# Differential attention interleaved with its projections: heads 0-3 between chunks, output product in contraction halves, bias sum and maximum in one operation

## What is computed

```python
proj = h @ w_in                                  # 1024 -> q, k, v of 1024 each
q = rms_norm(q.reshape(B, S, 8, 2, 64), g[0]) * 64 ** -0.5
k = rms_norm(k.reshape(B, S, 8, 2, 64), g[1])
p1 = softmax(einsum('bhqd,bhkd->bhqk', q1, k1) + bias)
p2 = softmax(einsum('bhqd,bhkd->bhqk', q2, k2) + bias)
out = einsum('bhqk,bhkv->bhqv', p1 - lam * p2, vh)
out = rms_norm(out, subln_g) * (1.0 - lam_init)  # over each head's 128 columns
return out.reshape(B, S, 1024) @ w_out           # added to x
```

## Time and profile before

| | us |
|---|---|
| median of 3 runs | 2019.35 |
| lowest and highest of them | 2018.79, 2026.88 |
| the profiled execution, its own time | 2024.16 |
| span of that execution, first to last instruction | 2022.4 |
| busy in the span: PE, DVE, ACT | 1924.5, 1226.9, 992.1 |
| mean granted TensorE clock | 0.986 |

### The profile page before, as it was taken

One profiled execution on the slowest core, in us unless ns is written; L12 is line 12 of the kernel. 1 busy time (PEld: TensorE's weight loads), 2 busy tenths in 40 slices (PEclk: granted clock), 3 DMA queues, 4 the chain that ended last, 5 costly groups with the idle time before them and its releaser, 6 DMA issues.

```text
span 2022.4 us, 26323 instructions
## 1 busy us (share of the span) xinstructions
PE 1924.5 (95%) x9384; PEld 1613.5 (80%) x9384; DVE 1226.9 (61%) x1633; ACT 992.1 (49%) x1479; POOL 64.2 (3%) x94
## 2 busy tenths in 40 slices
PE   9999989999999998799999999978989999989998
PEld 7887777888788886688888887867878788878886
DVE  5554786555555578655555566887565556655564
ACT  5444665544544455654453546633355543334444
POOL 1000000000000000000000001010000012100000
PEclk9999999999999999999999999989989999999999
DMA  7656334666685653166565555422135544336453
GB/s 224 188 185 185 120 115 153 184 188 188 189 257 186 186 172 125 57 184 182 189 200 167 183 167 176 148 77 70 40 107 170 159 146 126 104 105 210 153 187 115
DMA packets 215891, 316.88 MB, mean 157 GB/s; under 512 B 16658, under 2 KB 115208, under 8 KB 215536
## 3 DMA queue, kind: packets, MB, share of 16 engines
q1 hardware_dynamic: 212704, 306.76, 49.2%
q0 software_dynamic: 3024, 8.75, 1.3%
q10 hardware_dynamic: 64, 0.02, 0.0%
HBM read 314.41 MB, written 3.16 MB: 157 GB/s over the span
## 4 chain that ended last, share of the span: by engine, by line
PE 86%; DVE 8%; ACT 3%; issue 2%; DMA 0%; SPq 0%; DVEq 0%; ACTq 0%
PE acc L754 50%; PE acc L759 24%; PE tp L714 4%; DVE w_lo L1998 1%; PE tp L1163 1%; PE tp L870 1%; PE mx L1163 1%; DVE arena L2478 1%; ACT w_hi L1381 1%; DVE arena L2242 1%; PE mx L1302 1%; PE mx L1303 1%; DVE x L2069 1%; DVE arena L2402 1%; PE mx L1218 0%
## 5 line engine op out<-in xcount | busy, mean ns | idle before, releaser
L1998 DVE TENSOR_TENSOR w_lo<-w_raw,w_hi 128x1024 fp32r<-128x1024 f32 (+1 forms) x589 | 712.6, 1217 | 518.3 <-ACT w_hi L1381 516.3
L1381 ACT ACTIVATE w_hi<-w_raw 128x1024 fp32r<-128x1024 f32 (+1 forms) x589 | 612.9, 1048 | 568.7 <-PE acc L759 546.7
L754 PE MATMUL acc<-w_hi,norm_hi 128*128 128x512 f32 x1488 | 475.0, 401 | 4.1 <-DVE norm_lo L2017 3.5
L754 PE MATMUL acc<-w_hi,norm_lo 128*128 128x512 f32 x1488 | 461.8, 392 | 0.0
L759 PE MATMUL acc<-w_lo,norm_hi 128*128 128x512 f32 x1488 | 396.4, 389 | 0.0
L754 PEld LDWEIGHTS acc<-w_hi,norm_lo 128*128 128x128 f32 x1488 | 281.6, 190 | 59.8
L759 PEld LDWEIGHTS acc<-w_lo,norm_hi 128*128 128x128 f32 x1488 | 278.8, 188 | 58.0
L754 PEld LDWEIGHTS acc<-w_hi,norm_hi 128*128 128x128 f32 x1488 | 274.2, 191 | 58.9 <-issue 3.1
L754 PE MATMUL acc<-w_hi,inner_hi 128*128 128x512 f32 (+1 forms) x864 | 267.3, 391 | 4.0 <-DVE inner_lo L2017 2.5
L754 PE MATMUL acc<-w_hi,inner_lo 128*128 128x512 f32 (+1 forms) x864 | 262.9, 386 | 0.0
L759 PE MATMUL acc<-w_lo,inner_hi 128*128 128x512 f32 (+1 forms) x864 | 226.9, 385 | 0.0
(11 more groups left out here) (309 smaller groups left out, 1351.5 us busy)
## 6 DMA issues: line engine op xcount, KB each, us to landing
w_raw<-in_ffn_w_gu SPq DMA_DIRECT2D x352, 256.0 KB, 3.0
w_raw<-in_ffn_w_down SPq DMA_DIRECT2D x88, 512.0 KB, 4.6
w_raw<-in_pool_w_in SPq DMA_DIRECT2D x64, 512.0 KB, 3.8
w_raw<-in_gdn_w_in SPq DMA_DIRECT2D x48, 512.0 KB, 3.9
w_raw<-in_pool_w_out SPq DMA_DIRECT2D x32, 512.0 KB, 4.4
w_raw<-in_mla_w_in SPq DMA_DIRECT2D x26, 512.0 KB, 3.7
w_raw<-in_gla_w_in SPq DMA_DIRECT2D x24, 512.0 KB, 3.6
w_raw<-in_diff_w_in SPq DMA_DIRECT2D x24, 512.0 KB, 4.3
```

The source lines that it names most:

```text
L754: pe.matmul(acc_of(g, i, part, tok, 0, w), t[:, tile * SEQ + tok * P:tile * SEQ + (tok + 1) * P], b_hi, start=t is hi and k + kk == 0, sto ...
L1381: act.activation(slot(w_hi, g, i, p, 0, n), slot(w_raw, g, i, p, 0, n), ACT.Copy).then_inc(S["rounded"], 1)
L1998: dve.tensor_tensor(slot(w_lo, g, i, p, 0, n), slot(w_raw, g, i, p, 0, n), slot(w_hi, g, i, p, 0, n).bitcast(F32), ALU.subtract).then_inc( ...
```

## The change

`diff` now has six single blocks, q0, k0, v0, q1, k1, v1, where 0 are the columns of heads 0-3. After v0 the eight units of heads 0-3 run; PE puts one chunk of q1, k1 or v1 between the transposes and the values of each. The steps for q1 and k1 stand between the steps of these units on ACT and DVE. In this half there is one bank for scores and one shared by transposed probabilities and output. The output product is ordered by halves of the contraction: chunks 0 to 3 need heads 0-3 only. Heads 4-7 follow with three score banks; the roots, normalisation and transposes of the outputs are made for four heads at a time. The bias sum and the maximum become one operation for each of the two score matrices of a unit, which writes the negated sum and its minimum; the exponential takes scale -1. In the diff, cut to its core, "..." marks what is left out.

```diff
+        if turn_by is not None:
+            self.chunks.sort(key=lambda c: (c[1] // turn_by, c[0], c[1]))
...
+def halves(name, w, kt, cols, per, turn_by):
+
+    def source(first):
+        def piece(i, k, nk):
+            ap = w[k * P:(k + nk) * P, first:first + cols].rearrange("(t k) n -> k t n", k=P)
+            return [(lambda s: s[:, 0:nk * cols].rearrange("p (t n) -> p t n", t=nk), ap)]
+        return piece
+    return Gemm(name, 1, [(kt, cols, per, source(n * cols)) for n in range(2)], turn_by=turn_by)
...
-    return [linear("diff.qk", w, KD, BANK, 4, 2),
-            linear("diff.v", w, KD, BANK, 2, 2, first=2 * DM, evac="act_evac"),
-            linear("diff.out", t["diff_w_out"][0], KD, BANK, TT, 2)]
+    return [linear("diff.q0", w, KD, BANK, 1, 2),
+            linear("diff.k0", w, KD, BANK, 1, 2, first=DM),
+            linear("diff.v0", w, KD, BANK, 1, 2, first=2 * DM, evac="act_evac"),
+            linear("diff.q1", w, KD, BANK, 1, 2, first=BANK),
+            linear("diff.k1", w, KD, BANK, 1, 2, first=DM + BANK),
+            linear("diff.v1", w, KD, BANK, 1, 2, first=2 * DM + BANK, evac="act_evac"),
+            halves("diff.out", t["diff_w_out"][0], KD, BANK, 2, KD // 2)]
...
         def diff_bank(n):
 
-            return bank(mx, n % 4) if n % 4 < 2 else bank(tp, n % 4 - 2)
+            return bank(mx, 0) if n < diff_half else (bank(mx, 0), bank(tp, 0), bank(tp, 1))[(n - diff_half) % 3]
+
+        def diff_pt_bank(n):
+
+            return bank(mx, 1, 0, SEQ) if n < diff_half else bank(acc, 2 * G["diff.v1"].odd(0) + n % 2, 0, SEQ)
+
+        def diff_o_bank():
+
+            return bank(mx, 1, SEQ, P)
...
+            def finish_halves(g, xt, need):
+
+                st = following.get(g.name.split(".")[0])
+                for p in (g.n // 2, g.n // 2 + 1):
+                    product(g, 0, xt, part=0, only=p, need=need)
+                product(g, 0, xt, part=1, only=g.n - 2, need=need)
+                if st:
+                    turn_x(st, (0, 1))
+                product(g, 0, xt, part=1, only=g.n - 1, need=need)
...
                 def scores(n):
                     h, it = units[n]
-                    if n >= DIFF_AHEAD:
-                        pe.wait_ge(S["diff_s_taken"], n + 1 - DIFF_AHEAD)
+                    if 0 < n <= diff_half:
+                        pe.wait_ge(S["diff_s_taken"], n)
+                    elif n >= diff_half + 3:
+                        pe.wait_ge(S["diff_s_taken"], n - 2)
...
                 def probs_turned(n):
                     pe.wait_ge(S["diff_p_ready"], n + 1)
-                    if n >= 2:
+                    if 0 < n < diff_half:
+                        pe.wait_ge(S["diff_o_taken"], n)
+                    elif n >= diff_half + 2:
                         pe.wait_ge(S["diff_pt_ready"], n - 1)
                     for kt in range(TT):
-                        last = pe.transpose(bank(acc, n % 2, kt * P, P), p[:, n % 2 * SEQ + kt * P:n % 2 * SEQ + (kt + 1) * P], ident[:, :])
+                        last = pe.transpose(diff_pt_bank(n)[:, kt * P:(kt + 1) * P], p[:, n % 2 * SEQ + kt * P:n % 2 * SEQ + (kt + 1) * P],
+                                            ident[:, :])
                     see["diff_pt_turned"].up(last)
                 def values(n):
                     h, it = units[n]
                     pe.wait_ge(S["diff_pt_ready"], n + 1)
-                    if n >= 2:
-                        pe.wait_ge(S["diff_o_taken"], n - 1)
+                    if n >= diff_half:
+                        pe.wait_ge(S["diff_o_taken"], n)
                     for kt in range(TT):
-                        last = pe.matmul(bank(acc, 2 + n % 2, 0, P), pt[:, n % 2 * SEQ + kt * P:n % 2 * SEQ + (kt + 1) * P],
+                        last = pe.matmul(diff_o_bank(), pt[:, n % 2 * SEQ + kt * P:n % 2 * SEQ + (kt + 1) * P],
...
+                product(q0_g, 0, norm_t, need=need)
+                product(k0_g, 0, norm_t, between=lambda p: turn_block(0) if p == 2 else None)
+                product(v0_g, 0, norm_t, between=lambda p: turn_block(1) if p == 2 else None)
+                turned(see["tp_ready"].n - 1)
                 pe.wait_ge(S["diff_vec_ready"], 1)
+                scores(0)
+                product(q1_g, 0, norm_t, only=0)
+                wait_evacuated(pe, v0_g, 0)
+                filling = [*[(q1_g, p) for p in range(1, 4)], *[(k1_g, p) for p in range(4)], (v1_g, 0)]
+                for n in range(diff_half):
+                    if n + 1 < diff_half:
+                        scores(n + 1)
+                    probs_turned(n)
+                    g, p_n = filling[n]
+                    product(g, 0, norm_t, only=p_n)
+                    values(n)
+                    if n == 5:
+                        turn_block(2)
+                product(v1_g, 0, norm_t, only=1)
+                turn_heads(0)
+                product(v1_g, 0, norm_t, only=2)
+                turn_block(3)
+                product(v1_g, 0, norm_t, only=3)
+                turned(see["tp_ready"].n - 1)
+                for n in range(diff_half, diff_half + 3):
                     scores(n)
+                product(out_g, 0, inner_t, part=0, only=0, need=need_heads)
+                wait_evacuated(pe, v1_g, 0)
+                for n in range(diff_half, 2 * diff_half):
                     probs_turned(n)
+                    if n == diff_half + 1:
+                        product(out_g, 0, inner_t, part=0, only=1, need=need_heads)
+                    if n + 3 < 2 * diff_half:
+                        scores(n + 3)
+                    values(n)
+                product(out_g, 0, inner_t, part=1, only=2, need=need_heads)
+                product(out_g, 0, inner_t, part=1, only=3, need=need_heads)
+                turn_heads(1)
+                finish_halves(out_g, inner_t, need_heads)
...
+                plain_units(6)
+                feed.to(q1_g.chunk0 + 4)
+                exps(0)
+                for n in range(diff_half):
+                    take_probs(n)
+                    feed.to(q1_g.chunk0 + n + 5)
+                    if n + 1 < diff_half:
+                        exps(n + 1)
+                    if n == 3:
+                        block(2)
+                    if n == 4:
+                        block_root()
+                        act.activation(warm[:, :], eps[:, :], ACT.Exp)
+                    if n == 7:
+                        block(3)
+                    take_o(n)
+                root(0)
+                block_root()
+                act.activation(warm[:, :], eps[:, :], ACT.Exp)
+                feed.to(out_g.chunk0 + 1)
+                for u in range(2):
+                    hi_part(inner_t, 2 * u, lambda k: ROWS["subln"])
+                feed.to(out_g.chunk0 + 2)
+                plain_units(2)
+                feed.to(out_g.chunk0 + 3)
+                scaled_evac(v1_g, 0, diff_t["v"], DM, ACT.Copy, first=BANK)
+                for n in range(diff_half, diff_half + 3):
                     exps(n)
+                feed.to(out_g.chunk0 + 4)
+                for n in range(diff_half, 2 * diff_half):
                     take_probs(n)
+                    if n == diff_half + 1:
+                        feed.to(out_g.chunk0 + 5)
+                    if n + 3 < 2 * diff_half:
+                        exps(n + 3)
+                    if n + 3 == 2 * diff_half:
+                        act.activation(warm[:, :], eps[:, :], ACT.Sqrt)
+                    take_o(n)
+                root(1)
+                feed.to(out_g.chunk0 + 7)
+                for u in range(2, 4):
                     hi_part(inner_t, 2 * u, lambda k: ROWS["subln"])
+                finish_halves(out_g)
...
-                    b = bias[:, (it * DIFF_H + h) * SEQ:(it * DIFF_H + h + 1) * SEQ].rearrange("p (a k) -> p a k", a=1)
-                    dst = s[:, ring * BANK:(ring + 1) * BANK].rearrange("p (m k) -> p m k", m=2)
-                    see["diff_s_taken"].up(dve.tensor_tensor(dst, diff_bank(n).rearrange("p (m k) -> p m k", m=2),
-                                                             b.to_broadcast([P, 2, SEQ]), ALU.add))
-                    see["diff_s_taken"].wait(dve)
-                    see["diff_max_ready"].up(dve.tensor_reduce(stat[:, 16 + 2 * ring:18 + 2 * ring], dst, AX_X, ALU.max, negate=True))
+                    b = bias[:, (it * DIFF_H + h) * SEQ:(it * DIFF_H + h + 1) * SEQ]
+                    for m in range(2):
+                        last = dve.tensor_tensor_reduce(out=s[:, ring * BANK + m * SEQ:ring * BANK + (m + 1) * SEQ],
+                                                        in0=diff_bank(n)[:, m * SEQ:(m + 1) * SEQ], in1=b, scale=-1.0, scalar=3.0e38,
+                                                        op0=ALU.add, op1=ALU.min, accum_out=stat[:, 16 + 2 * ring + m:17 + 2 * ring + m])
+                    see["diff_s_taken"].up(last)
...
+                feed.before_evac(q0_g, 0)
+                evac(0)
```

(54 more changed lines are left out.)

210 lines of the change are left out of this document (94 added, 116 removed).

## The result

| | before | after |
|---|---|---|
| time, median (range) | 2022.5 us (2018.2 to 2026.9), 10 runs | 2031.0 us (2028.2 to 2040.3), 10 runs |
| ratio, 95% interval | | 1.0048 [1.0031, 1.0065] |
| span of the profiled execution | 2022.4 | 2027.6 |
| this stage in it | 144.07 | 154.60 |

The forecast was 2031. The change makes the kernel slower by 0.3 to 0.65%, 6 to 13 us. The interval lies on both sides of the 0.5% at which the prediction parted "slower" (chance 0.53) from "no change" (0.38), so which of the two it is stays open.

A forecast was written before the change was run, and what follows sets the result against it. PE bounds the kernel, so only its idle time can be won. Waits rise from 26.1 to 34.6 us (+8.5), clock adds 3.0: +11.5 on 2019.35 gives 2031, own range 2029.4 to 2034, wider range 2016 to 2038.

The forecast's parts named there:

- 2 unit 3 to 4: First half: PE waits 3.0 us for take_o(3), queued on ScalarE behind block(2), which waits for VectorE's evacuation.
- 3 unit 4 to 5: First half: PE waits 3.4 us for take_o(4), behind two table loads, a wait for P(5), and a root.
- 7 turn_block(3): Between the halves: the turning of block 3 and its copies make PE wait 1.1 us.
- units 8 to 12: Second half: a unit takes 3.6 us against 2.37, with 2.0 of waiting in each, 10.0 in all.
- last three units: End of second half: transposes, copy and values follow with nothing between, plus a 1.28 table load; waits 3.2 us.
- merged operation, S: VectorE's bias sum and maximum per unit, as two operations with accumulator reads: 1.1 us, between 0.8 and 1.7.
- clock: PE's clock falls after long waits, slowing work at turn_heads(0) and unit 8: adds 3.0 us, bounds 0 and 7.
- The 26.1 of before: Old kernel, last product chunk to first output product: 26.1 of 53.1 us is PE waiting or slow clock.
- drain behind a table load: ScalarE: the skill page's 1.38 drain per table load would add 4.1 us; left out of the sum; chance 0.02.
- The first: Rival: same waits, but the clock stays up or falls only inside waits; 2025.5 to 2027.9 us; chance 0.38.
- The third: Rival: first-half chunks really cover the blocks' steps; 2012.6 us, or 2006.4 with 2.37 per second-half unit; chance 0.09.
- The slow merged operation: Rival: VectorE's merged operation takes 1.7 us per unit, adding 5; 2036 us, or 2040 with more clock; chance 0.09.

The follow-up runs named there:

- e4: Changed kernel with ScalarE's take_o of units 3, 4 and 7 put ahead of the blocks' squares and root; 2027.6 us, ratio 1.0026, stage 151.6.
- e7: Changed kernel with its second half in the old unit order and the q1 and k1 blocks' steps moved among units 0 to 7; 2017.7 us, ratio 0.9961.
- e9: Changed kernel with matmuls that feed nothing put into PE's waits (11, 11 and 6 in each of units 10 to 15); 2030.2 us, ratio 1.0045.
- e11: Kernel of e7 with matmuls that feed nothing: 7 ahead of unit 8's turning, 8 among the last values; 2012.7 us, ratio 0.9955, stage 134.6.
- e5: Changed kernel with more matmuls that feed nothing in PE's waits (16, 16 and 8 in each of units 9 to 15); 2032.7 us, ratio 1.0045.
- e10: Kernel before with merged operation, root table loaded earlier, heads' normalisation split, and matmuls that feed nothing near the end; 2009.6 us, ratio 0.9934.
- e2: Kernel before the change with the merged operation alone; 2009.0 us, ratio 0.9934, stage 135.0.
- e12: The same kernel as e2, run again in another session; 2011.8 us, ratio 0.9951, stage 135.7.

## Why the prediction was right, and where its terms were not

The total was right, in part by luck: +11.5 forecast, +10.5 in the stage, a median of 2031.0 against 2031. By the medians the change cost only 8.5. That they still meet at 2031 is because the forecast was built on a median of 2019.35 over three runs, and the kernel before has 2022.5 over ten. Of the terms, too, some misses cancelled.

| step | forecast | measured |
|---|---|---|
| 1 before scores(0) | 2.5 | 2.16 |
| 2 unit 3 to 4 | 3.0 | 2.60 |
| 3 unit 4 to 5 | 3.4 | 3.15 |
| 4 turn_block(2) | 2.3 | 1.93 |
| 5 unit 7 | 0.8 | 0.72 |
| 6 turn_heads(0) | 3.2 | 2.92 |
| 7 turn_block(3) | 1.1 | none |
| 8 unit 8 | 3.4 | 2.82 |
| units 8 to 12 | 10.0 | 6.95 |
| last three units | 3.2 | 2.28 |
| end | 1.6 | 1.50 |
| plain units | 0.1 | 0 |
| all waits after | 34.6 | 27.0 |
| merged operation, S | 1.1 | 0.70 |
| clock | 3.0 | about 6 |

- **The list of places held.** Seven of the eight waits stood where the three queues laid side by side had put them, each 0.1 to 0.6 shorter than reckoned. e4 and e7 showed their causes: take `take_o` out from behind the block, or the block's work out from among the units, and the waits at those places go or shrink, in e4 by moving in part to the next one. Place 7 was wrong: neither the turning (810.34) nor the scores behind the next chunk (813.98) wait. The slow chunk ahead gave VectorE 1.7 us more; at full clock, in e9, 0.38 of a wait appears there.
- **S was mis-sized.** VectorE's rows for it are these:

```profile
815.04 0.42 DVE L2512 CUSTOM_DVE_ANT_0 arena<-mx,arena 128x256 f32<-128x256 f32 x1 [0.20 <-PE mx L1095]
815.39 0.08 DVE L2512 DVE_READ_ACCUMULATOR2_ANT stat<- 128x1 f32 x1
815.39 0.42 DVE L2512 CUSTOM_DVE_ANT_0 arena<-mx,arena 128x256 f32<-128x256 f32 x1
815.73 0.08 DVE L2512 DVE_READ_ACCUMULATOR2_ANT stat<- 128x1 f32 x1
```

  The second starts 0.35 after the first, with the accumulator read of 0.08 lying under it, so S is 0.70, below even my lower bound of 0.8. I had added 0.14 for a read that costs nothing. The loop's period was to be 3.6 and is 3.22, 0.4 less, just what S lacked. Waiting a unit is 1.47 where I had 2.0. Over five units the 0.4 is 2.0, half of the 4 us by which the second half was too dear. The Trainium skill's formula for fp32 tensor_tensor ("VectorE: DVE Perf Modes", the section on the TRN2 errata), (N + 151) / 0.96 ns, gives an estimated 424 ns for 256 elements; the row's length of 0.42 agrees, while the distance between starts is 0.35.
- **The clock was mis-sized the other way**, 3.0 against about 6, inside the bounds of 0 and 7. I had weighed the single waits of 3 us. The clock stayed up behind the waits of units 4 and 5 and fell behind the last three units, where no wait is over 1.3. PE's busy time doesn't foretell it either: it was 3.36 of 6 us there and 3.41 in the 6 us ahead, which had 1.00. The forecast's remark that a slower chunk behind unit 4 or 5 ends inside the next wait is what e9 did behind unit 5.
- **The base was mis-sized too.** The 26.1 of before held waits and slow or long work, while the stretches from 787.00 to 840.00 have 19.5 idle. So the base was 6.6 too high as waits and the waits of after 7.6 too dear, and the two nearly cancel, which is luck. Measured as differences over the stage, idle went up 7.5 (8.5 forecast) and busy 3.0 (3.0 forecast: some 6 of slow clock after, less what before had of it, such as the transposes of 1.97). How the 6.6 divides between the clock and operations that run to their full length where nothing follows (scores 1.03, not 0.87), I did not take apart.
- **No drain behind a table load.** 783.40 starts 0.01 after the load at 782.11 ends. The Trainium skill, "ScalarE: Activation LUTs", section What ACT_TABLE_LOAD costs, adds 1.38 there; here, too, the trace shows none.
- **The rivals.** The first (clock stays up, 2025.5 to 2027.9) is what e9 made, and its stage is 4.2 lower, which from 2031 would be 2027; its runs had 2030.2. The third (the chunks cover the blocks' steps, 2012.6) failed for the reason given, that `take_o` stands behind square and root. It is what e7 built, and with the second loop mended as well it came to 2017.7. The slow merged operation was ruled out.
- **What I left out.** The prediction priced the change as one thing. The merged operation alone in the kernel before, with S at 1.1, would have come to 16 x 0.22 = 3.5 us less; it was 9.1, with S at 0.70 and VectorE setting the pace of thirteen of its fifteen distances between units.

## What to carry to other kernels

Covering small attention work with product chunks pays only if nothing else stands in the in-order queues of the engines that feed it. List, for each unit, what is queued ahead of the step that frees the next buffer, and move squares, roots and table loads behind it. Where a change has two parts, price each in the old layout and in the new: a faster VectorE operation is worth nearly all that it saves in a loop that VectorE sets (0.54 of 0.62 us here) and nothing in one that a chunk sets. After the order is right, look at what runs behind a thinly used stretch, since the clock there can cost as much as a wait. Before a difference between two profiles is put down to an edit, look whether it lies where the edit is: 1.6 of e11's 4.4 did not.

## What the runs showed of the hardware

- The VectorE operation with accumulator (0.42 for 256 elements, PSUM and SBUF in, fp32) follows itself every 0.35 us, its accumulator read of 0.08 hidden.
- The clock doesn't follow the single wait: 1.00 behind one of 3.15 in after and 0.69 behind the same wait in e9, 1.00 behind scores(0)'s wait of 2.16 in after and 0.72 behind it (2.15) in e7, 0.61 behind one of 2.82 that follows some 17 us with another of 2.92, and 0.69 over 8 us behind units with no wait over 1.5. Matmuls that feed nothing, put into the waits, kept it at 0.99 (e9) to 1.00 (e5, e10, e11) over the stage. Part of that is chance: e11 also lacks a fall that e7 has ahead of all the matmuls put in. They have to fit: one of 128x128 by 128 columns in fp32 took 0.22 to 0.23 us (sixteen in 3.73 and eight in 1.95, e5).
- Outside the changed stage, executions of one and the same kernel differ by up to 8 us (e2 and e12). The granted clock differs there too: from 200 to 300 us, in the gla stage, it is 0.97 in e2 and 0.93 in e12. How much of the 8 us comes from the clock was not taken apart. Differences of under 5 us between kernels were settled by the stage, not by the run.
